# Inverting all chunks of a chunked RWKV-7 recurrence before its steps, and regrouping the products of a step

## The reference, cut to what matters

```python
def _wkv_step(S, inp):
    r_t, w_t, k_t, v_t, a_t, b_t = inp
    sa = jnp.einsum('bhvk,bhk->bhv', S, a_t)
    S = S * w_t[:, :, None, :] + sa[..., None] * b_t[:, :, None, :] + v_t[..., None] * k_t[:, :, None, :]
    y = jnp.einsum('bhvk,bhk->bhv', S, r_t)
    return S, y
```

## Time and profile before

| What | Value |
|---|---|
| Median of three runs (lowest, highest) | 2052.11 us (2051.4, 2058.19) |
| Profiled execution | 2060.91 us |
| Its span, first to last instruction | 2058.9 us |
| Mean granted TensorE clock | 0.914 of full speed |
| TensorE matmul busy | 1736.7 us (84%) |
| VectorE, ScalarE, GpSimd busy | 666.6, 427.5 and 71.3 us |

### The profile page before, as it was taken

One profiled execution on the slowest core, in us unless ns is written; L12 is line 12 of the kernel. 1 busy time (PEld: TensorE's weight loads), 2 busy tenths in 40 slices (PEclk: granted clock), 3 DMA queues, 4 the chain that ended last, 5 costly groups with the idle time before them and its releaser, 6 DMA issues. The chain is left out here.

```text
span 2058.9 us, 35738 instructions
## 1 busy us (share of the span) xinstructions
PE 1736.7 (84%) x15376; PEld 1242.2 (60%) x15376; DVE 666.6 (32%) x1533; ACT 427.5 (21%) x852; POOL 71.3 (3%) x76
## 2 busy tenths in 40 slices
PE   3687987999798798789898989979299999992797
PEld 2255865876585486467575755436188888881343
DVE  3124433533543343152424252225211111114343
ACT  2121122113113111031313131003101111112133
POOL 0000000000000000000000000000300000004000
PEclk8788998999899898899999999998699999996799
DMA  3011000000100100432323252007269999976211
GB/s 125 1 38 32 3 14 13 21 15 1 32 3 14 27 7 8 183 155 103 155 103 155 103 211 82 0 24 296 97 222 367 366 365 367 367 273 207 108 41 36
DMA packets 74543, 244.16 MB, mean 119 GB/s; under 512 B 13712, under 2 KB 36496, under 8 KB 64656
## 3 DMA queue, kind: packets, MB, share of 16 engines
q1 hardware_dynamic: 62000, 198.82, 26.2%
q0 software_dynamic: 7776, 26.23, 3.4%
q10 hardware_dynamic: 4608, 16.78, 2.0%
HBM read 210.00 MB, written 31.81 MB: 117 GB/s over the span
## 5 line engine op out<-in xcount | busy, mean ns | idle before, releaser
L387 PE MATMUL bank<-h,w 128*128 128x352 f32 (+1 forms) x576 | 184.5, 478 | 27.0 <-PEq L274 27.0
L387 PEld LDWEIGHTS bank<-h,w 128*128 128x128 f32 x576 | 110.2, 194 | 94.6 <-issue 32.2
L1768 DVE COPY xgT<-bank 128x512 f32<-128x512 f32 x64 | 41.2, 686 | 318.7 <-PE bank L1700 318.7
L1714 PEld LDWEIGHTS bank<-xgT,we_g 128*128 128x128 f32 x1024 | 121.4, 195 | 17.7 <-issue 14.4
L971 PE MATMUL bank<-h,wqkv 128*128 128x352 f32 (+1 forms) x384 | 119.4, 473 | 13.8 <-DMA wqkv<-in_wqkv 13.8
L1714 PE MATMUL bank<-xgT,we_g 128*128 128x128 f32 x1024 | 121.9, 278 | 2.8 <-DVE xgT L1768 2.8
L1714 PE MATMUL bank<-xgT,we_u 128*128 128x128 f32 x1024 | 119.6, 275 | 0.0
L1714 PEld LDWEIGHTS bank<-xgT,we_u 128*128 128x128 f32 x1024 | 116.9, 192 | 0.0
L1724 PE MATMUL bank<-we_d,hT 128*128 128x512 f32 x256 | 115.0, 592 | 0.0
L1911 PE MATMUL bank<-wp,unT 128*128 128x512 f32 x256 | 113.2, 601 | 0.0
L971 PEld LDWEIGHTS bank<-h,wqkv 128*128 128x128 f32 x384 | 73.4, 192 | 57.5 <-issue 15.1
(11 more groups left out here) (371 smaller groups left out, 2732.5 us busy)
## 6 DMA issues: line engine op xcount, KB each, us to landing
we_g<-in_weg SPq DMA_DIRECT2D x32, 1024.0 KB, 12.3
we_u<-in_weu SPq DMA_DIRECT2D x32, 1024.0 KB, 13.9
we_d<-in_wed SPq DMA_DIRECT2D x32, 1024.0 KB, 15.9
cache<-in_kcj SPq DMA_DIRECT2D x4, 5120.0 KB, 16.3
cache<-in_vcj SPq DMA_DIRECT2D x4, 5120.0 KB, 15.5
y_rows<-yo ACTq DMA_DIRECT2D x32, 512.0 KB
w<-in_win SPq DMA_DIRECT2D x15, 512.0 KB, 5.6
wqkv<-in_wqkv SPq DMA_DIRECT2D x4, 1536.0 KB, 19.1
```

The source lines that it names most:

```text
L387: mm = pe.matmul(out, w3[:, kd, q, :], g.uT[:, kd, a:a + w], start=(kd == 0), stop=(kd == KD - 1))
L1714: mm = pe.matmul(bank[2 + e % 2][:, 128 * (2 * a + f):128 * (2 * a + f) + CAP], w[:, k, 128 * f:128 * f + 128], xT[e % 2][:, k, :], start= ...
L1768: last = dve.tensor_copy(xT[e % 2][:, 4 * c:4 * c + 4, :].rearrange("p k q -> p (k q)"), bank[c][:, :])
```

## The change

All 17 chunks are inverted before the first step, as three subsets of 6, 6 and 5 chunks in 42 parts, each subset with two banks of its own. Between the parts stand 13 job pairs in banks 0 and 1, one after the first part of each triple. A job pair waits until both copies of the pair before it are done (`b_free0`, `b_free1`, in place of six semaphores, so 55 are cleared). In the even ones the products of the two heads of a chunk follow each other, each head to its own bank. The initialisation has three sets in place of four, in the banks of the inversion. In a step the product of the old state with the query side (L614) stands in `step_u` behind L599 and starts the sum; the 128-row product (L612) follows later and ends it. The state uses one bank (4), and VectorE no longer waits for `c_y` before it writes `st`. The three state products and the sample's product with `s0` all stand before step 0.

```diff
-            SUBS = [[(0, 5), (5, 5)], [(10, 4), (14, 3)]]
-            FIRST = 10
-            PARTS = 28
...
+            SUBS = [(0, 6), (6, 6), (12, 5)]
+            ZB, XB = (2, 4, 6), (3, 5, 7)
+            HOPS = 14
+            PARTS = 3 * HOPS
+            PIECES = [(0, 6), (6, 6), (12, 5)]
+            PAIRS = 13
+            kind_of = lambda k: ("z", "x", "t")[k // 3 % 3]
+            level = lambda k: k // 9
+            count = lambda k: 3 * level(k) + k % 3 + 1
+            pair_after = lambda k: k // 3 if k % 3 == 0 and k // 3 < PAIRS else None
...
-            sbank = lambda c: bank[3 - c // 4 % 2]
+            sbank = bank[4]
             SC = slice(448, 512)
+            free = (s["b_free0"], s["b_free1"])
+            turned_piece = lambda n: (PIECES[n][0], min(PIECES[n][1], NC - PIECES[n][0]))
...
+                    def job_pair(n):
+
+                        if n:
+                            pe.wait_ge(s["b_free0"], n)
+                            pe.wait_ge(s["b_free1"], n)
+                        if n < 10:
+                            q = n // 2
+                            for c in range(4 * q, min(4 * q + 4, NCH)):
+                                o = slice(128 * (c - 4 * q), 128 * (c - 4 * q) + 128)
+                                if n % 2 == 0:
+                                    for hh in range(2):
+                                        mm = pe.matmul(bank[hh][:, o], bk[hs(hh), c, :, :], ar[hs(hh), c, :, :], start=True, stop=True)
+                                else:
+                                    pe.transpose(bank[0][:, o], both(bk[:, c, :, :]), g.ident[:, :])
+                            if n % 2:
+                                for c in range(4 * q, min(4 * q + 4, NCH)):
+                                    o = slice(128 * (c - 4 * q), 128 * (c - 4 * q) + 128)
+                                    mm = pe.matmul(bank[1][64:128, o], v[:, c * CW:c * CW + CW], g.ident[:, :], start=True, stop=True)
+                            mm.then_inc(s["b_job"], 2)
+                            return
+                        for x in (2 * n, 2 * n + 1):
...
                     def step_u(c):
...
                             for hh in range(2):
-                                pe.matmul(sbank(c)[hs(hh), SC], g.ident[hs(hh), hs(hh)], st[hs(hh), c % 2, :], start=True, stop=False)
+                                pe.matmul(sbank[hs(hh), SC], g.ident[hs(hh), hs(hh)], st[hs(hh), c % 2, :], start=True, stop=False)
+                        if c >= 8 and c % 4 == 0:
+                            pe.wait_ge(s["c_yev"], c // 4 - 1)
+                        for hh in range(2):
+                            if c < NC:
+                                pe.matmul(yout(c, hh), st[hs(hh), c % 2, :], ar[hs(hh), c, 1, :], start=True, stop=False)
+                            else:
+                                pe.matmul(yout(c, hh), g.ident[hs(hh), hs(hh)], w0s[hs(hh), 1, :, :], start=True, stop=False)
 
                     def step_state(c):
...
                         for hh in range(2):
-                            o = yb[hs(hh), o0:o0 + CW]
-                            pe.matmul(o, uv[:, c, hh, :], gm[:, c, hh, CW:128], start=True, stop=False)
-                            if c < NC:
-                                mm = pe.matmul(o, st[hs(hh), c % 2, :], ar[hs(hh), c, 1, :], start=False, stop=True)
...
+                            mm = pe.matmul(yout(c, hh), uv[:, c, hh, :], gm[:, c, hh, CW:128], start=False, stop=True)
                         mm.then_inc(s["c_y"], 1)
...
+                    for k in range(PARTS):
+                        inverse_part(k)
+                        if pair_after(k) is not None:
+                            job_pair(pair_after(k))
+                    pe.wait_ge(s["b_xev"], 3 * 5)
+                    pe.wait_ge(s["b_free0"], PAIRS)
+                    pe.wait_ge(s["b_free1"], PAIRS)
+                    for i in range(3):
+                        state_products(i)
```

More of the change, by code:

```diff
@@ L552, in inverse_part @@
                                 else:
-                                    mm = pe.matmul(bank[4 + sub][hs(hh), o:o + CW], zb[hs(hh), c, :], xb[hs(hh), c, :], start=True, stop=True)
+                                    mm = pe.matmul(bank[ZB[sub]][hs(hh), o:o + CW], zb[hs(hh), c, :], xb[hs(hh), c, :], start=True, stop=True)
                         mm.then_inc(s["b_" + kind], 1)
[L556 to L560, removed]
-                            else:
[L562 to L571, removed]
@@ L679, in _ @@
                     pe.wait_ge(s["c_wtev"], 3)
[L680 removed]
+                    for c in range(NCH):
                         step_u(c)
[L682 removed]
+                        if c == 1:
                             pe.wait_ge(s["c_wev"], 1)
@@ L716, in _ @@
-                    turned(0)
-                    values(0)
-                    values(1)
-                    turned(1)
-                    values(2)
-                    products(0)
-                    products(1)
+                    for n in range(1, 10, 2):
+                        q = n // 2
+                        c0, c1 = 4 * q, min(4 * q + 4, NCH)
+                        act.wait_ge(s["b_job"], 2 * n + 2)
+                        act.activation(bkt[:, c0:c1, :, :].rearrange("p c h e -> p (c h e)"), bank[0][:, 0:128 * (c1 - c0)], ACT.Copy).then_inc(free[0], 1)
+                        act.activation(uv[64:128, c0:c1, :, :].rearrange("p c h e -> p (c h e)"), bank[1][64:128, 0:128 * (c1 - c0)], ACT.Copy).then_inc(free[1], 1)
@@ new lines, in _ @@
+                    for x in range(20, 26):
+                        c0, m = turned_piece(x - 20) if x < 23 else PIECES[x - 23]
+                        act.wait_ge(s["b_job"], x + 1)
+                        act.activation((wt if x < 23 else bv)[:, c0:c0 + m, :], bank[x % 2][:, 0:m * CW].rearrange("p (c x) -> p c x", c=m), ACT.Copy).then_inc(free[x % 2], 1)
+                    for i in range(3):
+                        c0, m = turned_piece(i)
+                        act.wait_ge(s["c_wt"], i + 1)
+                        act.activation(wt[:, c0:c0 + m, :], bank[ZB[i]][:, 0:m * CW].rearrange("p (c x) -> p c x", c=m), ACT.Copy).then_inc(s["c_wtev"], 1)
```

198 lines of the change are left out of this document (60 added, 138 removed).

## The result

The changed kernel takes 2002.1 us (median of four runs, 1995.5 to 2004.5) against 2051.8 for the kernel before on the same chip. The ratio is 0.9746 with a 95% interval of 0.9716 to 0.9776; applied to 2052.1 that is 2000 us, 52 less, where 39 were forecast and the range ended at 2001. Repeated beside later experiments it took 1995.9, ratio 0.9720 (0.9701 to 0.9739). The profiled execution took 2002.5 us (2060.9 before).

A forecast was written before the change was run, and what follows sets the result against it. TensorE's issue was taken to bound the inversion and mixed steps, a TensorE-copy-state chain the bare steps. Per stretch +2.0 and +1.5 in front, -13.5 in steps: -10.0; with semaphores 39 us, 2052.1 to 2013; range 2001 to 2033.

The forecast's parts named there:

- the hand-over inside a step: In a step, from the state's end to L591: 0.15 us, taken from the copy's end to L606.
- the charge for the half clock: Head of the inversion: 2.3 us per stretch, between nothing and the present 4.3.
- the sequence behind the last step: After the sixteen intervals: keeps its pace, set by VectorE's L813; four semaphores fewer save 0.2 us per block.
- rival 1: No half clock at all in the inversion: 4 x 2.3 us less, 2004 us; chance 0.14.
- The step: Sixteen step intervals: the chain decides, 1.55 us each, 24.8 in place of 38.3, so -13.5 per stretch.
- TensorE's work in front: Before the steps: inversion 29.8 us and jobs 15.6, 45.4 per stretch, then 0.8 to the state products.
- rival 3: Row halves don't overlap in the 64x128 job: 2.18 us, 4.9 per pair, 20 in all, 2033; chance 0.08.
- The rule against it: Frequent short idles between matmul groups make the clock fall: 17 bare steps in a row would drop to 1.2 GHz.
- rival 2: Clock falls to half after the first six bare steps: 0.45 us more per step, 20 in all, 2033; chance 0.12.
- Rivals 4 and 5: Job pairs wait for copies, 2085 us, chance 0.05; queue doesn't hold L591, steps stay 1.79, 2028 us, chance 0.06.
- the gain here and the cost in front belong together: Ten old steps carried 392 inversion instructions, so the steps' -13.5 us belongs with the +2.0 and +1.5 in front.

The follow-up runs named there:

- the grouped order: Changed kernel, but the old state's query products of both heads stand behind both 128-row products, still behind the wait for uv: 2007.3 us, ratio 0.9782.
- both reorderings: Kernel before with only the regrouped step and the alternating heads in the 64x128 job, inversion left in place: 1994.3 us, ratio 0.9701.

## Why the prediction was right or wrong

Direction and mechanism were right; the forecast gain was too small by 19 us in the profiles (58.2 to 39) and by 13 in the medians' ratio. What failed are two terms of the sum, the hand-over inside a step and the charge for the half clock, and one thing it took for unchanged, the sequence behind the last step. The range ended too high with them: its lower end is rival 1 with a step of 1.49, which comes to 2000 by its own terms and not 2001, and the step took less than that bound. Step by step:

- **The step.** Right that the queue held L591 and that a step becomes a chain without it. The term "0.15 (copy's end to L606, taken for state to L591)" was mis-sized: that hand-over takes 0.06 when the shape before it is the same. With 0.10 less in fifteen steps and 1.24 in the last interval, sixteen are 23.05, not 24.8: 7.0 us over four stretches, the largest error.
- **The half clock.** The charge of 2.3 per stretch was the other term far off. It cost 1.20 in two stretches and nothing in the other two, 2.4 in place of 9.2: 6.8 us. Rival 1 was half right, and its bound, nothing, would have been nearer than the middle. In how many heads the clock is at half varies from profile to profile.
- **TensorE's work in front.** 4.1 us too long over four stretches: the wait before the state products is 0.58, not 0.8, and the sum of parts and jobs was some 0.8 too high each. The even job's 1.09 was right, and so was the overlap argued from the earlier trace rows. Without alternation the job takes 1.63, not the 2.18 of rival 3, since half of it overlaps even so; that order cost 4.1 us over the four stretches, about 6.5 if the half clock had been alike in both. Against these three stands the initialisation, 0.2 to 1.2 longer up to the first z: 2.3 us. The prediction took the 5.4 of the first stretch for all four, but this part too is longer or shorter by its share of half clock, and the second stretch of the kernel before had 6.7 already. So 7.0 + 6.8 + 4.1 + 0.4 (the 3.3 for 3.4) - 2.3 = 16.0, the difference between 338.4 and 322.4.
- **Behind the last step.** "Keeps its pace" failed: L690 is on that path and ran at half clock; at full clock it takes 0.9 less, and the gaps gave 6.8 in place of 0.8. The clears were priced at their length of 0.044 us; 59 of them start from 173.9 to 178.0, so 0.07 apart, and four fewer in four places are 1.1 us.
- **The rule against it.** Sixteen bare intervals in a row held the clock at 1.00 in every stretch. The trace doesn't agree with the rule of the Trainium skill (TensorE: Matmul & The Clock Gate, "A second HAM failure mode: psum-queue depth-cycling") for the new order. For the old order, with the same inversion in front, it agrees in part: the clock fell in two stretches of four without any long gap, but didn't rise again within the steps. There it cost 14.4 us in the profile and 19 between the medians, which four products a step took back. So rival 2 rested on the right danger. The shorter step alone didn't keep clear of it, as the grouped order shows.
- **Rivals 4 and 5** are excluded by the timelines: behind the head TensorE is busy for 39.44 of 40.02 us, so no job pair stands waiting for a copy, and L613 is not held.
- **What was not seen:** "the gain here and the cost in front belong together" treated the move as a necessary part. The kernel with both reorderings and the move left out shows that it isn't.

Open: why the clock falls with the query products grouped behind the copy and not with them ahead of it, both at 1.45 us a step (filling the grouped order's waits, as was done for the old one, would have tested TensorE's longer idle time); and why joining the heads' job shortens the half-clock part in the kernel before.

## What to carry to other kernels

Look in the timeline for instructions that stand between a released operand and the product that uses it, and for tile shapes that alternate there: sorting them by shape took 28 us from the stretches here, a joint job of both array halves 33, and the large restructuring gave nothing beside them. Before adding idle time to TensorE in a chain, test the chain with a few products that nobody reads: if it gets faster, the clock was the loss. Price a disturbance that comes and goes (a half clock behind a wait) by both ends, not by the middle.

## What the runs showed of the hardware beyond that

- Eight 64x128 float32 products (sixteen instructions) take 1.09 us with the heads alternating over the array halves, 1.63 one head after the other in one job, where the second starts 0.55 us behind the first, and 2.18 in two jobs.
- A product on VectorE's fresh result starts 0.06 us behind it where the shape before it in the queue is the same (the state to L613, 248.34 to 248.40; L764 to L671, 260.34 to 260.40), and 0.14 where it changes (the copy's end to L633, 249.00 to 249.14).
- A chain of steps with TensorE busy for 22.89 of 27.97 us dropped to half clock in two of four equal stretches of one execution; with 26.58 of 27.97 it did in none of four.
- TensorE's backward branch of the loop takes 3.35 to 3.98 us where it is taken (0.08 where it isn't), that of the other engines 0.04 to 0.07.
